# Third block's convolution input by seven half-size products; in the layers, softmax behind a weight sum and half of the rotation behind the third gate

## What is computed

```python
for layer in range(2):                      # hybrid_layer
    h = rmsnorm(x, norm_w)
    proj = h @ w_in                         # 1024 -> 4360 columns, split in 15 parts
    ya = moba_attention(aq, ak, av) * silu(ag)          # 8 heads, causal, with ALiBi
    yb = head_norm(retention(rotate(bq), rotate(bk), bv)) * silu(bg)
    yc = head_norm(mlstm(silu(conv(cq, ck)), cv, ...) * sigmoid(co)) * silu(cg)
    x = x + concat(ya, yb, yc) @ w_out
x = rmsnorm(x, final_norm_w)

xn = rms_norm(x, norm1_g)                   # the third block
h_in = xn @ w_in_2                          # q, k, v, lru_x, lru_gate
attn = block_attention(rope(rms_norm(q)), rope(rms_norm(k)), v)
xc = centred_depthwise_conv(lru_x, conv_w, conv_b)      # 4 taps
lru = (rglru(xc, forward) + rglru(xc, backward)) * gelu(lru_gate)
x = x + concat(rms_norm(attn), rms_norm(lru)) @ w_out_2
x = x + moe_ffn(rms_norm(x, norm2_g))       # 4 of 32 experts per token
```

## Time and profile before

| | us |
|---|---|
| median of 3 runs (lowest to highest) | 1391.94 (1390.69 to 1393.55) |
| time of the profiled execution | 1392.25 |
| its span, first to last instruction | 1390.1 |
| PE busy | 1181.6 (85%) |
| DVE busy | 668.3 (48%) |
| ACT busy | 210.0 (15%) |
| DMA rate, mean over the span | 337 GB/s |

### The profile page before, as it was taken

The page is one execution under the profiler, slowest core; times in us unless marked ns, Lnnn a source line. Parts: engine busy times, 40 slices in busy tenths (PEclk is TensorE's granted clock), DMA queues, the critical chain, the costliest instruction groups (busy, mean ns, idle before and its releaser), DMA issues.

```text
span 1390.1 us, 28188 instructions
## 1 busy us (share of the span) xinstructions
PE 1181.6 (85%) x10350; PEld 628.0 (45%) x10351; DVE 668.3 (48%) x1443; ACT 210.0 (15%) x474; POOL 49.4 (4%) x84
## 2 busy tenths in 40 slices
PE   7999999999999989966786879877899987878565
PEld 7868588775774333422332324333334432333222
DVE  4668474775587445433443434433453543434323
ACT  1223021231163111010010101101110110101001
POOL 0000000001012000000000000000000000000000
PEclk9999999999999999989999999999999999999879
DMA  9943188131724999999999999999979999999997
GB/s 352 280 145 99 55 302 167 69 114 67 273 114 172 397 417 406 429 430 428 428 427 430 430 428 428 426 429 430 428 314 430 428 430 428 428 429 428 430 427 296
DMA packets 63078, 467.83 MB, mean 337 GB/s; under 512 B 6848, under 2 KB 11708, under 8 KB 38460
## 3 DMA queue, kind: packets, MB, share of 16 engines
q1 hardware_dynamic: 58556, 462.49, 80.7%
q10 hardware_dynamic: 3856, 2.65, 2.3%
q0 software_dynamic: 624, 2.10, 0.4%
HBM read 465.12 MB, written 1.05 MB: 335 GB/s over the span
## 4 chain that ended last, share of the span: by engine, by line
PE 55%; DMA 33%; DVE 6%; issue 3%; ACT 1%; ACTq 1%; SPq 1%; POOL 0%; POOLq 0%; DVEq 0%
DMA ring<-in_w_up_dram 30%; PE bank L1519 18%; PE bank L1043 6%; PE bank L1550 6%; PE bank L1050 5%; PE bank L1265 3%; PE bank L1162 3%; PE bank L1166 3%; DMA ring<-in_w_down_dram 3%; PE bank L1567 2%; PE bank L1500 2%; PE bank L1463 1%; PE bank L1531 1%; PE bank L1324 1%; ACTq L985 1%
## 5 line engine op out<-in xcount | busy, mean ns | idle before, releaser
L1519 PE MATMUL bank<-ring,mem 128*32 128x512 f32 x2688 | 376.5, 653 | 122.8 <-DMA ring<-in_w_up_dram 100.4
L1519 PEld LDWEIGHTS bank<-ring,mem 128*32 128x32 f32 x2688 | 103.9, 118 | 303.3 <-issue 247.7
L1550 PE MATMUL bank<-ring,mem 128*32 128x256 f32 x2560 | 155.3, 382 | 5.5 <-DMA ring<-in_w_down_dram 5.0
L1000 ACT ACTIVATE const<-bank 64x512 f32<-64x512 f32 x46 | 27.3, 594 | 795.3 <-PE bank L1519 795.3
L2634 DVE TENSOR_TENSOR mem<-bank,const 64x512 f32<-64x512 f32 x45 | 30.7, 682 | 216.4 <-PE bank L1519 216.4
L1043 PE MATMUL bank<-ring 128*128 128x256 f32 x512 | 112.6, 380 | 0.0
L1550 PEld LDWEIGHTS bank<-ring,mem 128*32 128x32 f32 x2560 | 75.4, 110 | 74.2 <-issue 26.3
L1043 PEld LDWEIGHTS bank<-ring 128*128 128x128 f32 x512 | 96.8, 190 | 13.7 <-issue 1.0
L1519 PE MATMUL bank<-x_mem,mem 128*32 128x512 f32 x256 | 70.7, 702 | 30.5 <-DMA ring<-in_w_up_dram 30.5
L2628 DVE TENSOR_TENSOR mem<-bank,const 128x256 f32<-128x256 f32 x45 | 19.8, 439 | 144.8 <-PE bank L1500 144.8
L1567 PE MATMUL bank<-mem,cg 32*128 32x256 f32 x784 | 70.0, 426 | 5.0 <-DVE mem L2681 4.9
(11 more groups left out here) (453 smaller groups left out, 1421.0 us busy)
## 6 DMA issues: line engine op xcount, KB each, us to landing
ring<-in_w_up_dram SPq DMA_DIRECT2D x64, 2048.0 KB, 28.7
ring<-in_w_gate_dram SPq DMA_DIRECT2D x54, 2048.0 KB, 32.1
ring<-in_w_down_dram SPq DMA_DIRECT2D x53, 2048.0 KB, 27.0
ring<-in_w_in_dram SPq DMA_DIRECT2D x19, 2048.0 KB, 13.0
x_mem<-in_w_gate_dram SPq DMA_DIRECT2D x10, 2048.0 KB, 32.2
x_mem<-in_w_down_dram SPq DMA_DIRECT2D x10, 2048.0 KB, 28.9
ring<-in_w_out_dram SPq DMA_DIRECT2D x6, 2048.0 KB, 13.9
ring<-in_w_in_dram SPq DMA_DIRECT2D x2, 1056.0 KB, 6.3
```

What stands on the lines that cost most here:

```text
L1000: A(u_sb, UB[2 * T:4 * T, :], ACT.Copy).then_inc(ex["uc"], 1)
L1519: i = mm(gate_up_bank(q), xT[:, at:at + T], w[q // 2][:, c, 512 * (q % 2):512 * (q % 2 + 1)], start=(h == 0 and c == 0 and not begun), sto ...
L1550: i = mm(YB[quarter[q], 0:QD], hT_sb[:, at:at + T], w[:, c, cols_of[q]], start=(h == 0 and c == 0), stop=(h == 1 and c == 3), skip_group_c ...
```

## The change

Three edits.

1. **Third block.** `group2(0, "T", 2)` becomes `seven_products(0, DEPTH)`, with `sum_rows`, the four `mix` steps, `fold_most` and `fold_last` on DVE and `keep_first`, `keep_corner` on ACT in place of the two plain copies. The scaling of `x` stands between T1 and T4; the decays' steps stand behind `fold_most(0)`, so that Ln and the take-outs of k and v on ACT wait for it too. PE waits for C11 and C21 ahead of the gates' products, DVE ahead of the convolution.
2. **Layers, group 7.** T2 stands ahead of `a_softmax(2)`, T1 and T4 behind it as before.
3. **Layers, end.** `a_normalise(3)` first, then the first multiplication of the rotation, `fold_last(8)`, `a_gate(1)`, `a_turned(2)`, and only then the second multiplication and the rotation's sum.

Besides, ACT waits for its own copy of C11 before it counts two banks as used. Helper functions get the layer as an argument, which changes no instruction.

```diff
-SEVEN = {g: n for n, g in enumerate((1, 4, 7, 8))}
+SEVEN = {1: 0, 4: 1, 7: 2, 8: 3, 0: 0}
+PER_LAYER = 4
+FIRST_UNIT = {1: 2, 4: 8, 7: 14, 8: 16, 0: 2}
...
+        products_of[0] = lraw[:, :, 2:2 + S]
...
                     if g not in ROW_FORM:
+                        act.wait_ge(kept, seven(KEPT, l, g, "C11"))
                         act.sem_inc(pj_used, 2)
...
+            keep_first(0, DEPTH)
             arg2()
             A(lam(1), lam(0), ACT.Exp).then_inc(act_res, 1)
             arg2()
...
                 used2(A(v2[:, c, :], b[:, P:2 * P], ACT.Copy))
-            for c in range(2):
-                b = unit2(2 + c)
-                used2(A(lraw[:, 2 * c:2 * c + 2, 2:2 + S], ...
+            keep_corner(0, DEPTH)
...
-            group2(0, "T", 2)
+            seven_products(0, DEPTH)
             group2(2, "tok", 4)
+            pe.wait_ge(kept, seven(KEPT, DEPTH, 0, "C11"))
+            pe.wait_ge(folded, seven(FOLDED, DEPTH, 0, "C21"))
             pe.wait_ge(lru_w_in, 16 * 8)
             pe.wait_ge(xc_ready, 1)
...
                 a_turned(0)
+                mix(7, l, "T2")
                 a_softmax(2)
-                mix_rest(7)
-                fold_most(7)
+                mix(7, l, "T1")
+                mix(7, l, "T4")
+                fold_most(7, l)
...
+                a_normalise(3)
                 v.wait_ge(kept, seven(KEPT, l, 7, "C11"))
                 v.wait_ge(folded, seven(FOLDED, l, 7, "C21"))
                 table = lambda n: K(n).unsqueeze(1)
                 st.go(tt(rotB, rawB, table("ret_cos").to_broadcast([P, 4, S]), ALU.mult))
+                fold_last(8, l)
+                a_gate(1)
+                a_turned(2)
                 v.wait_ge(swapped_ready, 2 * l + 2)
-                st.go(tt(swapB, swapB, table("ret_sin").to_broadcast([P, 4, S]), ALU.mult))
-                a_normalise(3)
-                st.wait()
+                st.do(tt(swapB, swapB, table("ret_sin").to_broadcast([P, 4, S]), ALU.mult))
                 tt(rotB, rotB, swapB, ALU.add).then_inc(rotB_ready, 1)
-                fold_last(8)
-                a_gate(1)
                 v.wait_ge(rotB_ready, l + 1)
-                a_turned(2)
...
+            v.wait_ge(tr_used, DEPTH * TR_L + 6)
+            sum_rows(row_sums, DEPTH)
             st.go(v.memset(lraw[:, :, 0:2], 0.0))
...
+            arg2(tt(lam(0), lam(0), col("lam", 0, 8), ALU.min))
+            for name in ("T3", "T2", "T1"):
+                mix(0, DEPTH, name)
             for c in range(TC):
                 i = stt(out=x[:, c, :], in0=x[:, c, :], scalar=small[:, 32 + 2 * c:33 + 2 * c], in1=roww[:, :], op0=ALU.mult,
...
-            arg2(tt(lam(0), lam(0), col("lam", 0, 8), ALU.min))
+            mix(0, DEPTH, "T4")
+            fold_most(0, DEPTH)
+
             result2()
...
-            v.wait_ge(pj_used, DEPTH * PJ_L + 4)
+            fold_last(0, DEPTH)
+            v.wait_ge(kept, seven(KEPT, DEPTH, 0, "C11"))
+            v.wait_ge(folded, seven(FOLDED, DEPTH, 0, "C21"))
```

More of the change, by code:

```diff
@@ L81, in seven @@
 def seven(steps, l, g, name):
-    return (l * len(SEVEN) + SEVEN[g]) * len(steps) + steps[name]
+    return (l * PER_LAYER + SEVEN[g]) * len(steps) + steps[name]
 def mixed_through(l, g, name):
-    return l * len(MIX_ORDER) + MIX_ORDER.index((g, name)) + 1
+    return l * len(MIX_ORDER) + MIX_ORDER.index((g or 1, name)) + 1
 A_STEPS = 4
@@ L1919, in _, with sum_rows @@
                 hT0, hT1 = hT[:, :, 0:P], hT[:, :, P:S]
-                def sum_rows(sums, done):
+                def sum_rows(sums, l, done=0):
                     s1, s2, s3, s4 = sums
@@ L1931, in _, with mix @@
                 v.wait_ge(tr_used, l * TR_L + 5)
-                sum_rows(row_sums, 0)
-                def mix(g, name):
+                sum_rows(row_sums, l)
+                def mix(g, l, name):
                     b11, b12 = weights_of(g, 0, 0), weights_of(g, 0, 1)
@@ L1951, in mix, with mix_rest, fold @@
                     v.wait_ge(mixed, mixed_through(l, g, name))
-                def mix_rest(g):
+                def mix_rest(g, l):
                     for name in ("T2", "T1", "T4"):
-                        mix(g, name)
-                def fold(g, product, dst, b, other):
+                        mix(g, l, name)
+                def fold(g, l, product, dst, b, other):
                     if product == "M4":
-                        v.wait_ge(pj_ready, l * PJ_L + PJ_0 + 2 * g + 2)
+                        v.wait_ge(pj_ready, l * PJ_L + PJ_0 + FIRST_UNIT[g] + 2)
                     else:
@@ L1962, in fold, with fold_most @@
                     return tt(dst, chunks_of(b, g), other, ALU.add).then_inc(folded, 1)
-                def fold_most(g):
+                def fold_most(g, l):
                     m, e, f = banks_of(g)[1:]
@@ L2037, in _ @@
                 v.wait_ge(tr_used, l * TR_L + 7)
-                mix(4, "T3")
-                mix_rest(4)
-                fold_most(4)
-                fold_last(4)
+                mix(4, l, "T3")
+                mix_rest(4, l)
+                fold_most(4, l)
+                fold_last(4, l)
                 v.wait_ge(row_spread, 16 * C_HEADS * (l + 1))
@@ L2116, in _ @@
                 st.do(gated(flat, eC[:, :, 0:256], flat))
-                sum_rows(late_row_sums, 4)
-                mix(7, "T3")
-                mix(8, "T3")
+                sum_rows(late_row_sums, l, 4)
+                mix(7, l, "T3")
+                mix(8, l, "T3")
                 a_softmax(1)
@@ L2130, in _ @@
                 a_normalise(2)
-                fold_last(7)
+                fold_last(7, l)
                 a_gate(0)
@@ L2134, in _ @@
                 a_softmax(3)
-                mix_rest(8)
-                fold_most(8)
+                mix_rest(8, l)
+                fold_most(8, l)
+                a_normalise(3)
                 v.wait_ge(kept, seven(KEPT, l, 7, "C11"))
```

61 lines of the change are left out of this document (30 added, 31 removed).

## The result

| | before | changed kernel |
|---|---|---|
| median, us (lowest to highest) | 1391.93 (1390.67 to 1393.55), 6 runs | 1386.04 (1383.2 to 1386.59), 6 runs |
| ratio, 95% interval | | 0.995 (0.9939 to 0.9961) |
| profiled execution, its span | 1392.25, 1390.1 | 1386.36, 1384.1 |

The change gains 5.9 us; 5.0 were predicted. The time lies in the range that was given, but the forecast as a ratio, 1386.9 / 1391.94 = 0.9964, lies just outside the measured interval. The sign and the mechanisms hold; a size does not.

A forecast was written before the change was run, and what follows sets the result against it. PE was taken to bound the kernel ahead of the experts, the weight stream the experts' part. 0.55 + 3.2 - 0.05 + 1.3 = 5.0 us off 1392.25 gave 1387.25, as a median 1386.9 us; range 1385.0 to 1389.8.

The forecast's parts named there:

- Gain: 0.27 us a layer: Group 7 in the layers: T2 ahead of the softmax removes M6's idle, 0.55 us in all.
- Gain: 1.60 us a layer: Layer's end: an earlier gate removes PE's whole wait before the output projection, 3.2 us in all.
- the 0.05 that I took off without need: Layers: the two gains' 3.75 us taken as 3.7, since a wait rarely shrinks to exactly nothing.
- M5 needs it ... leaves 0.4 us: Group 7: T1 ends near 281.2, M5 needs it at 281.6, so 0.4 us are left.
- The gate is 0.3 us early: Layer's end: the gate is done about 303.3, before PE ends its transposes at 303.6.
- 0.8 us of margin: Layer's end: the rotation's sum ends about 306.8, PE reaches the scores that need it at 307.6.
- Edit 1, 12.5 us: Third block: the seven-product group takes 12.5 us instead of 13.81, a gain of 1.3 us.
- the 0.43 above it are small waits between products: Third block: pure column time is 12.08 us; the 0.43 us beyond it were put down to small waits.
- The weight loads: Third block: loads run beside matmuls; the rival of exposed loads, 21.5 us instead of 12.5, gave 1395.9 us, chance 0.01.
- The granted clock of 1.00: Layers ahead of the experts: PE was taken to run at its higher clock level, 2.4 GHz.
- The code fetch rival: Experts' loop: PE's 13.0 us of waits for "issue" double and lie open, giving 1399.9 us; chance 0.06.
- An experts' part of the same length: Experts' part: starts 5 us earlier with its length unchanged; a difference over 1 us would make the prediction wrong.

The follow-up runs named there:

- the two copies: Changed kernel with two more multiplications of `swapB` by 1.0 ahead of the rotation's second multiplication in each layer; single time 1390.91 us, a layer 164.13 us.
- edit 3 alone: Kernel before with only the new order at the layer's end; single time 1394.12 us beside 1392.78 for the kernel before, a layer 163.87 us.
- the third block alone: Kernel before with only the third block's `seven_products` edit; 1390.53 us, ratio 0.998.
- the layer edits alone: Kernel before with only the two layer edits, T2 ahead of the softmax and the new order at the layer's end; 1389.51 us, ratio 0.9975.

## Why the prediction was right in its parts and short in its size

- **The step that failed: the size of the layer terms.** "Gain: 0.27 us a layer" and "Gain: 1.60 us a layer" were taken from the idle times in brackets. Start to start, the gaps were 0.51 (M1 to M2, 9.54 against 9.03) and 1.77 (transposes to projection, 2.49 against 0.72), and these are what the edits gave, alone (0.53, 1.79) and together (2.32 a layer). The front part says that matmul ends are modelled and overlap the next start, and the prediction used that for the group of products (13.81, not 13.98), but not for the gaps. The listed idle begins at a modelled end; a run that goes on without a wait has its next start before that end. In the changed kernel line 1123 has a length of 0.88 and the next row starts 0.72 after it: 0.16 of overlap, the difference of 1.77 and 1.60 within 0.01. The Trainium skill says in "Perfetto Trace Analysis", "Tensor Engine Instruction (MATMUL, LD_WEIGHTS)", that the profiler works the end of a TensorE instruction out from its size; the trace agrees, by those 0.16 us. At M6 the overlap is 0.16 too, and a second cost comes to it, which no listed idle time holds: M6's second matmul starts 0.185 us after its first, where the others of the group start 0.11 apart, 0.07 more; that makes 0.50 of the 0.51. For two layers this is 2 x (0.24 + 0.17) = 0.82 us, and with the 0.05 that I took off without need, 0.87: the sum comes to 5.9, and the time to 1386.0.
- **"M5 needs it ... leaves 0.4 us"** held, with 0.26 left: T1 ends at 278.25, which is the forecast 281.2 less the 2.99 us by which the second layer starts earlier (185.31 to 182.32), and M5 starts at 278.51 without a wait.
- **"The gate is 0.3 us early"**: 0.18. **"0.8 us of margin"** at the rotation: 0.65, by the two copies. Both thin, both enough.
- **Edit 1, 12.5 us**: 12.50. But "the 0.43 above it are small waits between products" is wrong: no idle stands in the group. Its 112 matmuls of 128 columns start 0.112 us apart all through, where half of the 0.216 between two of 256 columns is 0.108, and that makes the 0.4; so the bound of 1.7 us "(no waits)" rested on waits that aren't there. Each margin held: the fold of C22 ends at 359.03, 10.1 us after the group's first product (10.0 forecast: 362.7 less 352.66), and M4 does not wait for it. ACT's take-outs waited for PE, not for the DMA issues. The copies of k and v end at 360.35, 1.1 ahead of the q group (0.9 predicted). The convolution starts at 362.27, 0.8 us behind the group's end (0.5 forecast), with the q group's 13.90 us over it.
- **The weight loads.** In the third block's new group 112 loads take 190 to 192 ns each and lie in 12.50 us. By the rule of the Trainium skill ("TensorE: Matmul & The Clock Gate", "The mechanism") that loads overlap with matmuls only when their row groups differ, these full-row loads should have been exposed, 21.5 us; the runs disagree with it at a second place. The same page of the Trainium skill names, in that section too and under "Step-by-step: what each phase is for", a second case in which a load is pulled ahead, that it goes to the background weight buffer. The trace agrees as far as it shows loads beside matmuls, 21.5 us of them in 12.50; where they went no run here shows. I should have weighed both cases.
- **The granted clock of 1.00**, taken for all that leads up to the experts: right in the profile I read, not in seven of twelve. The prediction had no term for it, 1.5 to 1.7 us in such an execution, and it carries over to the first request.
- **The code fetch rival** fell: the experts' loop waits 13.6 us for "issue" where it was 13.0, and the part's length is within its own scatter.
- **"An experts' part of the same length"**: 955.94 against 956.9, and 955.5 in the kernel before's second profile. My bound of 1 us on that was narrower than the scatter of one kernel.

## What to carry to other kernels

Size a gap of PE from start to start, against the same pair of rows where there is no gap, and not by the idle time listed before a row: a gap of 0.27 us was worth 0.51. When several parts change, cut the executions at fixed events and keep a ledger of the distances, since two profiles can agree with a sum whose terms are wrong. And ahead of a stage that streams weights, a microsecond more on the engine whose work releases its requests is about a microsecond later at the end, even where that engine waits many times behind it.

## What the runs showed of the hardware beyond that

- TensorE's clock fell to its lower level around two gaps of 1.27 and 0.83 us in seven executions and stayed up in four with the same gaps: 0.50 against 1.00 in the two microseconds around 341 us, 1.5 to 1.7 us longer.
- Around 1000 us the stream of weights pauses: SP's next request waits 39.9 us for a product of PE. How much arrives from 990 to 1035 us differs between executions. The kernel before, then edit 3 alone:

```profile
990.00:1035.00 45.00, 39.18 (x370) 13.90 (x366) 17.74 (x37) 7.50 (x16) 0.40 (x1) 0.94 0.81 339
```

```profile
990.00:1035.00 45.00, 37.55 (x346) 13.32 (x338) 17.11 (x35) 7.43 (x16) 0.40 (x1) 0.92 0.77 319
```

  At a granted clock of 0.94 PE does 370 matmuls in it and 339 GB/s arrive, at 0.92 it does 346 and 319 arrive. In six executions at 0.92 it was 319 to 340 GB/s, in two at 0.97 and 1.00 it was 359 and 360. But the length of the whole experts' part does not follow that clock: it is 959.9 us for edit 3 alone, 956.4 for the third block alone, both at 0.92, and 957.4 for the layer edits alone at 1.00. What sets its scatter stays open.
- A DVE operation with a scalar over 1024 columns took 0.68 to 0.69 us, one with a second tensor 1.23 (the copies of `swapB` and the rotation behind them).
